# The first weight tile of the output projections: all rounded parts first, then all rests

## The chip, the core and the metric

The kernel runs on one core of a Trainium2 chip. Its engines are TensorE (PE: matmuls, with weight loads shown apart as PEld), VectorE (DVE), ScalarE (ACT), GpSimd (POOL) and SyncE (SP, which issues the loads). Each engine works through its own list of instructions in order and waits on semaphores for the others. The metric is the device time of one execution in microseconds (us); the kernel before takes 3476.52 us, the median of 3 runs (3475.16 to 3477.75).

## The reference, cut to what matters

The reference is two transformer blocks of two layers each, on 512 tokens of width 1024; the second block also carries 256 context tokens. Each of the four layers has a mixer (attention heads in layers 0, 2 and 3, a gated delta rule in layer 1), an output projection, and a feed-forward part:

```
mixed = concat(heads) @ w_out          # 1024 x 1024, in every layer
x = x + gate * mixed
h = rmsnorm(x, g) * (1.0 + scale) + shift
x = x + gate_f * swiglu(h, w_in, w_out)
```

The change touches only `concat(heads) @ w_out`. In layers 2 and 3 two of the eight head chunks are normalised before it (the differential attention's `rmsnorm_2(o, subln_g)`). In layer 2 the projection is done for the 512 tokens and the 256 context tokens, in the others for the 512 tokens.

## The kernel before, in words

Activations lie with their features on the 128 partitions: eight chunks ("heads" in the code, each 128 features) of 512 or 768 token columns. The weights of an output projection come in four tiles of 1024 x 256, each giving two blocks (j = 0 and 1) of 128 output features.

A product of full precision is made from rounded numbers. Each operand is split into a rounded part (HI) and a rest (LO), and three products are added up in one PSUM bank: HI·HI, HI weight · LO activation, LO weight · HI activation. ACT writes the rounded parts (weights `W_HI`, heads `O_HI`), POOL subtracts to get the rest of the weights (`W_LO`), DVE to get the rest of the heads (`O_LO`). One (head, j) pair thus costs three matmuls of 128x512; one weight tile for 512 tokens is 8 x 2 x 3 = 48 of them.

The first tile (m = 0) of a projection is special, since the heads have only just been computed. ACT takes it in four pieces (`PIECES`): it rounds a quarter of the weight tile (line 555), then the two heads that go with it (line 526), four times over; in layers 2 and 3 the normalisation of heads 4 and 5 lies between the first piece and the second (lines 2875 and 2876 on ACT, 2882 on DVE, after sums on PE at line 2866). After the last head ACT loads another function table (line 529) and rounds the second tile (line 378), POOL then takes that tile's rest (line 390). DVE splits the heads in the same order (line 589), POOL the four weight pieces (line 565). PE runs `pe_out`: for each group of `side_by_side` heads it first issues the HI·HI products (line 483), each head behind a wait for `heads_rounded`, and then the two products with rests (lines 493 and 494), each head behind waits for the weight piece's rest (`piece_split`, for the last two heads `tile_split`) and for `heads_split`. In the delta rule's layer (`gdn_out`) the group is all eight heads, in the other three projections (`attn_out`, `out2`, `out3`) it is two.

In `out2` the 256 context columns of tile 0 follow by `pe_three` (lines 434 to 436, matmuls of 128x256). Tiles 1 to 3 use `pe_three` for everything, behind a wait for their own `tile_split`. When tile m is done, DVE adds it into X (line 601) and ACT rounds tile m + 2 into the buffer that has come free; squares of X (line 804 on ACT, sums at line 814 on POOL) feed the next norm, whose last sums are made by PE (line 826).

Of the kernel before, what the change touches and what calls it, by code (L numbers as in the profile page):

```python
# [15 lines left out]
DC = D // P  # L16
# [76 lines left out]
def build_program(nc, w_tiles, d_tiles, xT, ctxT, positions, consts, params, rope_tables, outT):  # L93
# [12 lines left out]
    with ctx:  # L106
# [90 lines left out]
        def sig(name):  # L197

            if name not in scratch:
                scratch[name] = sem(name)  # L200
            return scratch[name]
# [60 lines left out]
        def base(who, name, count):  # L262


            key = (who, name)
            at = BASE.get(key, 0)
            BASE[key] = at + count
            return at
# [159 lines left out]
        def pe_three(pe, o, w, hi, lo, x_hi, x_lo, n, wait=None):  # L428


            for k in range(n):
                if wait:
                    wait(k)
                pe.matmul(PS[:, o:o + w], hi(k), x_hi(k), start=k == 0, stop=False)  # L434
                pe.matmul(PS[:, o:o + w], hi(k), x_lo(k), start=False, stop=False)  # L435
                mm = pe.matmul(PS[:, o:o + w], lo(k), x_hi(k), start=False, stop=k == n - 1)  # L436
            return mm
# [22 lines left out]
        def heads_order(name):  # L460

            return [0, 1, 2, 3, 6, 7, 4, 5] if name in ("out2", "out3") else list(range(DC))

        def pe_out(pe, name, segs):
            e0 = E0[name]
            b_r = base("pe", "heads_rounded", DC)
            b = base("pe", "heads_split", DC)
            b_p = base("pe", "piece_split", PIECES - 1)
            heads = heads_order(name)
            side_by_side = DC if name == "gdn_out" else 2  # L470
            col = lambda k, j: slice(k * 256 + j * P, k * 256 + (j + 1) * P)
            for m in range(OWN[name]):
                hi, lo = W_HI[:, (SPLIT[name] + m) % 2, :], W_LO[:, (SPLIT[name] + m) % 2, :]
                pe.wait_ge(evac_done, e0 + m - 1)
                later = segs
                if m == 0:

                    (c0, w), later = segs[0], segs[1:]
                    for p0 in range(0, DC, side_by_side):
                        for p in range(p0, p0 + side_by_side):  # L480
                            pe.wait_ge(sig("heads_rounded"), b_r + p + 1)
                            for j in range(2):
                                pe.matmul(PS[:, out_column(m, j, c0):out_column(m, j, c0) + w], hi[:, col(heads[p], j)],
                                          O_HI[:, heads[p], c0:c0 + w], start=p == 0, stop=False)
                        for p in range(p0, p0 + side_by_side):
                            if p // 2 < PIECES - 1:
                                pe.wait_ge(sig("piece_split"), b_p + p // 2 + 1)
                            else:
                                pe.wait_ge(sig("tile_split"), SPLIT[name] + 1)
                            pe.wait_ge(sig("heads_split"), b + p + 1)  # L490
                            for j in range(2):
                                to = PS[:, out_column(m, j, c0):out_column(m, j, c0) + w]
                                pe.matmul(to, hi[:, col(heads[p], j)], O_LO[:, heads[p], c0:c0 + w], start=False, stop=False)
                                mm = pe.matmul(to, lo[:, col(heads[p], j)], O_HI[:, heads[p], c0:c0 + w], start=False,
                                               stop=p == DC - 1)
                                if p == DC - 1 and not later:
                                    mm.then_inc(tile_done if j else sig("out_first_done"), 1)
                    if not later:
                        continue
                else:  # L500
                    pe.wait_ge(sig("tile_split"), SPLIT[name] + m + 1)
                for j in range(2):
                    for c0, w in later:
                        mm = pe_three(pe, out_column(m, j, c0), w, lambda k: hi[:, col(k, j)], lambda k: lo[:, col(k, j)],
                                      lambda k: O_HI[:, k, c0:c0 + w], lambda k: O_LO[:, k, c0:c0 + w], DC)
                    mm.then_inc(tile_done if j else sig("out_first_done"), 1)
            pe_norm_sum(pe, OUT_SUM, sum(w for _, w in segs))
# [4 lines left out]
        def out_column(m, j, c0):  # L512
            return (m % 2) * 1536 + (1024 + j * 256 if c0 else j * 512)
# [302 lines left out]
        def pe_norm_sum(pe, o, w):  # L816
            n = base("pe", "norm_summed", 1)
            for last in range(2):
                if last:
                    pe.wait_ge(sig("norm_squared"), (n + 1) * DC)  # L820
                else:
                    pe.wait_ge(sig("norm_added"), (n + 1) * (DC - 2))
                src = NORM_SQ[:, (DC - 1) % 2, :] if last else NORM_SUM[:, :]
                for c in range(0, w, 512):
                    x = min(512, w - c)
                    mm = pe.matmul(PS[:, o + c:o + c + x], ones, src[:, c:c + x], start=not last, stop=bool(last))
            mm.then_inc(sig("norm_summed"), 1)
# [2130 lines left out]
        def _(pe):  # L2958
            ph = Phase()
            for layer in range(4):  # L2960
                segs = SEG1 if layer < 2 or layer == LAST else SEG2
                if layer == 0:
                    pe_ada0(pe)
                    pe_attn_in(pe)
                    ph.end(pe)
                    pe_stick(pe)
                    ph.end(pe)
                    pe_pairs(pe, causal_tasks())
                    ph.end(pe)
                    pe_out(pe, "attn_out", SEG1)  # L2970
                elif layer == 1:
                    pe_gdn_in(pe)
                    ph.end(pe)
                    pe_gdn_prep(pe)
                    ph.end(pe)
                    pe_gdn_inverse(pe)
                    ph.end(pe)
                    pe_scan(pe)
                    ph.end(pe)
                    pe_gdn_out(pe)  # L2980
                    pe_out(pe, "gdn_out", SEG1)
                else:
                    pe_in(pe, layer)
                    ph.end(pe)
                    pe_conv_norm(pe, layer)
                    ph.end(pe)
                    pe_pairs(pe, mixer_tasks(layer))
                    ph.end(pe)
                    pe_sub_norm(pe, layer)
                    pe_out(pe, f"out{layer}", segs)  # L2990
# [341 lines left out]
```

## Time and profile before

| | us |
|---|---|
| median of 3 runs (range) | 3476.52 (3475.16 to 3477.75) |
| the profiled execution | 3475.19 |
| its span in the trace | 3473.5 |
| PE busy | 3235.7 (93% of the span) |
| DVE, ACT, POOL busy | 1675.4, 1166.2, 1312.2 |
| granted TensorE clock over the span | 0.966 |

Of the profiled time 1.7 us lie outside the span. The granted clock is a share of 2.4 GHz: 1.00 is that level, 0.50 is 1.2 GHz, and a value between is a stretch with both. A matmul's row shows its whole passage; back to back they start closer together than they last, so a run of them is read from start to start. PE is the engine that is busy nearly always. The first tiles of the four projections begin at 342.69, 1160.45, 2032.01 and 3042.21 us of the span.

### The profile page before, as it was taken

What the parts mean: (1) busy time and instruction counts of PE and PEld (TensorE: products, weight loads), DVE (VectorE), ACT (ScalarE), POOL (GpSimd) and SP (SyncE); (2) the same over time, 40 slices, a digit from 0 to 9 for tenths busy, and PEclk for the clock granted to TensorE, in tenths of its full rate; (3) what the DMA queues carried; (4) which work ended last, traced back from release to release, by engine and by line L of the source; (5) the groups of instructions that cost most, each with busy time, mean ns of one, the idle gap of its engine ahead of it and who ended that gap; (6) DMA issues with size and microseconds to landing.
All of it is one profiled execution on the core that took longest, in us unless ns stands there. A gap on an engine that the chain in (4) does not pass through costs nothing. (4 is left out here: it accounts for less than half of the span.)

```text
span 3473.5 us, 43878 instructions
## 1 busy us (share of the span) xinstructions
PE 3235.7 (93%) x16780; PEld 2547.3 (73%) x16780; DVE 1675.4 (48%) x2845; ACT 1166.2 (34%) x1526; POOL 1312.2 (38%) x711
## 2 busy tenths in 40 slices
PE   7998999999976899998997998999999997989998
PEld 6864788878866688886883367888899783368887
DVE  5544442427566474654736625734355737431111
ACT  2244322223362322223234433222344325442222
POOL 3313444444461333433314543343400414544443
PEclk9989999999997899999998999999999998999999
DMA  6510243432201134432110022444344210022321
GB/s 261 192 63 25 109 182 139 189 119 85 72 1 49 61 145 151 169 149 75 62 37 1 1 73 87 173 146 182 139 172 161 92 49 1 25 85 82 106 86 66
DMA packets 54643, 352.91 MB, mean 102 GB/s; under 512 B 5856, under 2 KB 6880, under 8 KB 19552
## 3 DMA queue, kind: packets, MB, share of 16 engines
q1 hardware_dynamic: 54208, 348.79, 27.2%
q8 instruction: 100, 1.64, 0.2%
q10 hardware_dynamic: 288, 2.10, 0.2%
q14 instruction: 47, 0.39, 0.0%
HBM read 348.77 MB, written 2.10 MB: 101 GB/s over the span
## 5 line engine op out<-in xcount | busy, mean ns | idle before, releaser
L390 POOL TENSOR_TENSOR W_LO<-ring,W_HI 128x2048 fp32r<-128x2048 f32 (+1 forms) x177 | 729.4, 4121 | 1063.7 <-ACT W_HI L378 1063.7
L446 PE MATMUL PS<-H_HI,W_HI 128*128 128x512 f32 (+1 forms) x1888 | 712.2, 377 | 28.9 <-DVE H_LO L867 22.0
L448 PE MATMUL PS<-H_HI,W_LO 128*128 128x512 f32 (+1 forms) x1888 | 702.7, 372 | 0.0
L447 PE MATMUL PS<-H_LO,W_HI 128*128 128x512 f32 (+1 forms) x1888 | 702.5, 372 | 0.0
L378 ACT ACTIVATE W_HI<-ring 128x2048 fp32r<-128x2048 f32 (+1 forms) x214 | 366.3, 1712 | 471.2 <-PE PS L436 417.8
L446 PEld LDWEIGHTS PS<-H_HI,W_HI 128*128 128x128 f32 x1888 | 359.2, 190 | 93.0 <-issue 31.5
L448 PEld LDWEIGHTS PS<-H_HI,W_LO 128*128 128x128 f32 x1888 | 358.7, 190 | 63.0
L447 PEld LDWEIGHTS PS<-H_LO,W_HI 128*128 128x128 f32 x1888 | 359.1, 190 | 59.4 <-issue 0.2
L909 DVE SCALAR_TENSOR_TENSOR PS<-ring,SC,PS 128x256 f32<-128x256 f32 x768 | 376.2, 490 | 27.0
L434 PE MATMUL PS<-HID_HI,W_HI 128*128 128x512 f32 (+1 forms) x880 | 325.3, 370 | 4.9 <-DVE W_LO L390 4.0
L436 PE MATMUL PS<-HID_HI,W_LO 128*128 128x512 f32 (+1 forms) x880 | 323.8, 368 | 0.0
L435 PE MATMUL PS<-HID_LO,W_HI 128*128 128x512 f32 (+1 forms) x880 | 323.7, 368 | 0.0
L640 ACT ACTIVATE GATED<-PS 128x512 f32<-128x512 f32 (+1 forms) x110 | 61.1, 555 | 724.8 <-PE PS L448 724.8
L655 DVE TENSOR_TENSOR HIDDEN<-GATED,PS 128x512 f32<-128x512 f32 (+1 forms) x110 | 69.8, 634 | 424.6 <-ACT GATED L640 424.6
L784 DVE SCALAR_TENSOR_TENSOR X<-PS,MOD,X 128x512 f32<-128x512 f32 (+1 forms) x80 | 55.7, 696 | 386.0 <-PE PS L436 386.0
L434 PE MATMUL PS<-H_HI,U_HI 128*128 128x512 f32 x520 | 206.0, 396 | 19.5 <-DVE H_LO L867 14.0
L435 PE MATMUL PS<-H_LO,U_HI 128*128 128x512 f32 x520 | 204.7, 394 | 0.0
L436 PE MATMUL PS<-H_HI,U_LO 128*128 128x512 f32 x520 | 204.4, 393 | 0.0
L434 PEld LDWEIGHTS PS<-HID_HI,W_HI 128*128 128x128 f32 x880 | 165.9, 189 | 34.5 <-DVE W_LO L390 5.3
L436 PEld LDWEIGHTS PS<-HID_HI,W_LO 128*128 128x128 f32 x880 | 165.9, 188 | 27.7
L435 PEld LDWEIGHTS PS<-HID_LO,W_HI 128*128 128x128 f32 x880 | 165.9, 189 | 27.2
L2521 POOL TENSOR_TENSOR U_LO<-ring,U_HI 128x1024 fp32r<-128x1024 f32 x40 | 102.7, 2570 | 214.5 <-ACT U_HI L2509 214.5
(393 smaller groups left out, 5387.6 us busy)
## 6 DMA issues: line engine op xcount, KB each, us to landing
ring<-w_tiles SPq DMA_DIRECT2D x271, 1024.0 KB, 4.8
ring<-d_tiles SPq DMA_DIRECT2D x80, 704.0 KB, 4.1
X<-xT SPq DMA_DIRECT2D x1, 2048.0 KB, 12.5
WORK<-rope_tables ACTq DMA_DIRECT2D x2, 1024.0 KB, 4.9
outT<-H SPq DMA_DIRECT2D x8, 256.0 KB, 2.2
X<-ctxT SPq DMA_DIRECT2D x1, 1024.0 KB, 9.1
CN<-consts SPq DMA_DIRECT2D x1, 931.0 KB, 15.3
PR<-params SPq DMA_DIRECT2D x1, 465.5 KB, 3.5
```

The lines of the kernel that those rows point to most:

```text
L378: act.activation(W_HI[:, b, 0:w], ring[:, g % SLOTS, 0:w], ACT.Copy).then_inc(sig("tile_rounded"), 1)
L390: eng.tensor_tensor(W_LO[:, b, 0:w], ring[:, g % SLOTS, 0:w], W_HI[:, b, 0:w].bitcast(F32), ALU.subtract).then_inc(sig("tile_split"), 1)
L434: pe.matmul(PS[:, o:o + w], hi(k), x_hi(k), start=k == 0, stop=False)
L435: pe.matmul(PS[:, o:o + w], hi(k), x_lo(k), start=False, stop=False)
L436: mm = pe.matmul(PS[:, o:o + w], lo(k), x_hi(k), start=False, stop=k == n - 1)
L446: pe.matmul(to, hi[:, cols(k, j)], x_hi(k), start=k == 0, stop=False)
L447: pe.matmul(to, hi[:, cols(k, j)], x_lo(k), start=False, stop=False)
L448: mm = pe.matmul(to, lo[:, cols(k, j)], x_hi(k), start=False, stop=k == n - 1)
L640: act.activation(GATED[:, v, 0:w], PS[:, v * 1024:v * 1024 + w], ACT.Silu).then_inc(sig("gate_silu"), 1)
L655: dve.tensor_tensor(HIDDEN[:, v, 0:w], GATED[:, v, 0:w], PS[:, v * 1024 + 512:v * 1024 + 512 + w], ALU.mult).then_inc(evac_done, 1)
L909: ins = dve.scalar_tensor_tensor(out=out, in0=w, scalar=c[:, k:k + 1], in1=acc, op0=ALU.mult, op1=ALU.add)
L2521: pool.tensor_tensor(U_LO[:, i % 2, :].rearrange("p (k c) -> p k c", k=DC), half_source(layer, t, j), U_HI[:, i % 2, :].rearrange("p (k c) ...
```

## The change

In all four projections the group of heads of tile 0 is now all eight. The number of matmuls, their operands and what they add up to stay as they are; only their order on PE and the places of PE's waits differ, and only in `attn_out`, `out2` and `out3`.

```
             heads = heads_order(name)
-            side_by_side = DC if name == "gdn_out" else 2
+            side_by_side = DC
             col = lambda k, j: slice(k * 256 + j * P, k * 256 + (j + 1) * P)
```

PE's list in `out2`, before, from the sums of the sub-norm (line 2866) to the third head's rounded part; in brackets stands what an instruction waits for:

```order
L2866 MATMUL PS<-BIG,CN 128x256
L483 MATMUL PS<-O_HI,W_HI 128x512 [waits heads_rounded,evac_done]
L483 MATMUL PS<-O_HI,W_HI 128x512
L483 MATMUL PS<-O_HI,W_HI 128x512 [waits heads_rounded]
L483 MATMUL PS<-O_HI,W_HI 128x512
L493 MATMUL PS<-O_LO,W_HI 128x512 [waits heads_split,piece_split]
L494 MATMUL PS<-O_HI,W_LO 128x512
...
L483 MATMUL PS<-O_HI,W_HI 128x512 [waits heads_rounded]
```

Where the dots stand are six more products with rests: eight of them lie between the rounded parts of the second head and of the third. The same place after the change, to the first product with a rest:

```order
L2866 MATMUL PS<-BIG,CN 128x256
L483 MATMUL PS<-O_HI,W_HI 128x512 [waits heads_rounded,evac_done]
L483 MATMUL PS<-O_HI,W_HI 128x512
L483 MATMUL PS<-O_HI,W_HI 128x512 [waits heads_rounded]
L483 MATMUL PS<-O_HI,W_HI 128x512
...
L493 MATMUL PS<-O_LO,W_HI 128x512 [waits heads_split,piece_split]
L494 MATMUL PS<-O_HI,W_LO 128x512
```

Where the dots stand are the twelve rounded products of the third to the eighth head, each head behind its own wait for `heads_rounded`. The number of instructions is the same; the lists of DVE, ACT, POOL and SP are the same row for row.

## Rows read from the trace of the kernel before

**Rows 1.** The page: the span, and the granted clock in 40 slices.

```profile
span 3473.5 us, 43878 instructions
PEclk9989999999997899999998999999999998999999
```

**Rows 2.** Timeline, PE, out2: start, length, engine, line, operands [idle before <-releaser].

```profile
2032.01 1.63 PE L483 MATMUL PS<-O_HI,W_HI 128*128 128x512 f32 x4
...
2035.69 1.47 PE L483 MATMUL PS<-O_HI,W_HI 128*128 128x512 f32 x4 [0.22 <-ACT O_HI L526]
...
2037.53 0.47 PE L493 MATMUL PS<-O_LO,W_HI 128*128 128x512 f32 x1 [0.37 <-DVE O_LO L589]
...
2039.50 0.47 PE L493 MATMUL PS<-O_LO,W_HI 128*128 128x512 f32 x1 [0.82 <-DVE O_LO L589]
...
2046.13 0.28 PE L434 MATMUL PS<-O_HI,W_HI 128*128 128x256 f32 x1
```

**Rows 3.** Timeline, ACT, DVE and POOL, out2.

```profile
2034.81 1.56 ACT L526 ACTIVATE O_HI<-H 128x768 fp32r<-128x768 f32 x2
...
2035.67 8.25 DVE L589 TENSOR_TENSOR O_LO<-H,O_HI 128x768 fp32r<-128x768 f32 x6 [0.24 <-ACT O_HI L526]
...
2038.79 1.56 ACT L526 ACTIVATE O_HI<-H 128x768 fp32r<-128x768 f32 x2
2038.96 1.54 POOL L565 TENSOR_TENSOR W_LO<-ring,W_HI 128x512 fp32r<-128x512 f32 x1 [0.43 <-ACT W_HI L555]
...
2043.67 4.73 POOL L390 TENSOR_TENSOR W_LO<-ring,W_HI 128x2048 fp32r<-128x2048 f32 x1 [3.17 <-ACT W_HI L378]
```

**Rows 4.** Timeline, PE, gdn_out: first product with a rest, and tile 1's first.

```profile
1165.05 0.39 PE L493 MATMUL PS<-O_LO,W_HI 128*128 128x512 f32 x1
...
1172.30 0.39 PE L434 MATMUL PS<-O_HI,W_HI 128*128 128x512 f32 x1
```

**Rows 5.** Windows, tile 1 of out2: us, busy of PE, PEld, DVE, ACT, POOL, PEclk, DMA, GB/s.

```profile
2051.80:2068.00 16.20, 16.20 (x95) 14.28 (x94) 2.19 (x4) 3.40 (x3) 6.43 (x2) 1.00 0.24 83
```

**Rows 6.** Timeline, PE, the norm behind out2.

```profile
2106.07 2.93 PE L826 MATMUL PS<-NORM_SUM,CN 128*128 128x512 f32 x4 [3.99 <-POOL NORM_SUM L814]
```

**Rows 7.** Timeline, PE, ACT and POOL, attn_out.

```profile
342.69 1.66 PE L483 MATMUL PS<-O_HI,W_HI 128*128 128x512 f32 x4 [3.55 <-ACT O_HI L526]
...
346.62 1.14 ACT L526 ACTIVATE O_HI<-H 128x512 fp32r<-128x512 f32 x2
...
351.07 4.90 POOL L390 TENSOR_TENSOR W_LO<-ring,W_HI 128x2048 fp32r<-128x2048 f32 x1 [2.53 <-ACT W_HI L378]
...
355.44 0.39 PE L494 MATMUL PS<-O_HI,W_LO 128*128 128x512 f32 x1
...
356.12 0.47 PE L434 MATMUL PS<-O_HI,W_HI 128*128 128x512 f32 x1 [0.29 <-POOL W_LO L390]
```

**Rows 8.** Timeline, ACT, POOL and PE, out3.

```profile
3048.15 1.13 ACT L526 ACTIVATE O_HI<-H 128x512 fp32r<-128x512 f32 x2
...
3052.60 4.59 POOL L390 TENSOR_TENSOR W_LO<-ring,W_HI 128x2048 fp32r<-128x2048 f32 x1 [2.68 <-ACT W_HI L378]
...
3055.14 0.39 PE L494 MATMUL PS<-O_HI,W_LO 128*128 128x512 f32 x1
...
3057.33 0.47 PE L434 MATMUL PS<-O_HI,W_HI 128*128 128x512 f32 x1 [1.80 <-POOL W_LO L390]
```

**Rows 9.** Timeline, PE: two pauses of nearly one length.

```profile
1228.26 1.05 PE L925 MATMUL PS<-SM,ACC 128*128 128x1 f32 x8 [2.75 <-DVE ACC L909]
...
2132.41 1.05 PE L925 MATMUL PS<-SM,ACC 128*128 128x1 f32 x8 [2.59 <-DVE ACC L909]
```

**Rows 10.** Windows: behind these two pauses, and one of out2.

```profile
1230.60:1234.00 3.40, 3.40 (x9) 2.63 (x8) 3.15 (x8) 0.66 (x1) 2.66 (x1) 0.50 0.96 359
...
2131.70:2140.00 8.30, 7.59 (x37) 6.44 (x38) 6.99 (x15) 2.44 (x2) 4.50 (x1) 1.00 0.64 247
...
2039.00:2040.00 1.00, 0.50 (x2) 0.48 (x3) 1.00 (x2) 1.00 (x2) 1.00 (x1) 1.00 0.00 0
```

## The prediction, made before the changed kernel ran

> **What bounds the kernel now.** I read the page first. PE is busy 93% of the span and its clock is near the upper level almost everywhere [rows 1], so what counts is PE's own list: a microsecond that PE loses is lost, unless it would have waited anyway. The change touches three places of that list, so I then read the timeline of each, PE beside ACT, DVE and POOL. Three questions are put to each place: when does tile 0 end now, what paces it, and what does tile 1 wait for?
>
> The clearest place is out2, in layer 2 [rows 2, 3]. PE has the first two heads' rounded products out of the way by 2033.6 (2032.01 + 1.63). Then ACT is held up by the norm of heads 4 and 5, and the third head is rounded only at about 2035.6: L526 starts at 2034.81 and takes 1.56 for two heads. PE fills that hole with the eight rest products of the first two heads, and its wait before 2035.69 is 0.22 us. It has two more waits, 0.37 and 0.82 us, both for the rests of heads from DVE. The whole of tile 0 for 512 columns takes from 2032.01 to 2046.13, 14.1 us.
>
> **What 48 matmuls cost.** The delta rule's projection already runs the new order, but there all heads are rounded by the time PE comes. From its first rest product to tile 1's first product are 7.25 us for 32 matmuls, without a gap [rows 4], or 0.227 us each at the upper clock. So 48 need 10.9 us, and tile 0 of out2 now loses 3.2 us to waits and to the lower clock at its start.
>
> **The change, part by part.** No instruction is added or removed, and the four other engines keep their lists. PE's rest products move behind all rounded products. So the new order has a simple lower end: tile 0 can't end before (the last head is rounded) + 2 rounded products + 32 rest products, since the rest products, 7.25 us of work, now all stand behind the wait for the eighth head. A matmul starts 0.10 us behind the rounding that it waits for (2035.59 to 2035.69, rows 2 and 3).
>
> Out2: the last head is rounded at 2038.79 + 1.56 = 2040.35 [rows 3]. Then 0.10 + 2 x 0.227 + 7.25 = 7.8 us, so the rest products end at 2048.15, where before the next work began at 2046.13 [rows 2]. That is +2.0 us. The rests are not late in that sum: POOL has the last weight piece at 2038.96 + 1.54 = 2040.5, and DVE the last head at 2035.67 + 8.25 = 2043.92, while PE asks for it 28 products behind the start of the rest products, at about 2047. Nothing covers the 2.0 us. The 256 context columns follow at once in either kernel, and in tile 1 PE is busy for the whole 16.20 of 16.20 us [rows 5]: it doesn't wait there for POOL, whose W_LO is ready at 2043.67 + 4.73 = 2048.4 [rows 3]. Behind out2 comes the norm, a strict chain from PE over DVE, ACT and POOL back to PE [rows 6], which moves as a whole. What the later end of tile 0 holds up on the other engines is the addition into X and the rounding of tile 2, both 2.0 us later; tile 2 is wanted a whole tile later, some 16 us on.
>
> Attn_out: the last head is rounded at 346.62 + 1.14 = 347.76, and 7.8 us more give 355.56. Before, the last product of tile 0 started at 355.44 and its successor could start at 355.67, but tile 1 begins at 356.12, because POOL has its rest only at 351.07 + 4.90 = 355.97 [rows 7]. Both orders end ahead of that, so the change is worth 0, and with the same reason nothing could be gained there.
>
> Out3: the last head at 3048.15 + 1.13 = 3049.28, and 7.8 us more give 3057.08. Before, tile 0's products were through at 3055.14 + 0.23 = 3055.37, so tile 0 gets 1.7 us longer. But tile 1 waits for POOL until 3052.60 + 4.59 = 3057.19 and starts at 3057.33 [rows 8]: PE's wait of 1.80 us covers it, with 0.25 us to spare. Here 0. If that cover were gone, it would cost 1.7. Tile 2 is rounded 1.7 us later and is again wanted a whole tile (10.9 us) later, when ACT and POOL need under 7 for it.
>
> The three sums together give +2.0 us: 3475.19 + 2.0 = 3477.2 for the profiled execution. That one stood 1.33 below the median of the three runs, so as a median I say 3476.52 + 2.0 = 3478.5 us, or +0.06%. The runs of before spread over 2.6 us; 0.2%, 7 us, is about what a measurement of this kernel can tell from no change.
>
> **What the trace does not show** is PE's clock under the new order. In out2 PE will pause from 2033.6 to 2035.7 and then get two matmuls (0.45 us of work) at a time, about every 0.8 us with longer gaps between pairs of heads, until 2040.4. Two rows bound it. A pause of 2.59 us left the clock at 1.00 for what followed, a pause of 2.75 us of the same instruction brought it to 0.50 from 1230.60 to 1234.00 [rows 9, 10]. So a fall costs up to 3.4 us at half the pace, 1.7 us, and it may cost nothing if it lies where PE waits for heads. For the sum I take the clock held, as the new pause (2.1 us) is the shorter and as the clock stayed at 1.00 in out2 with PE half idle from 2039 to 2040 [rows 10]. Both ends, 0 and 1.7 us for each of out2 and out3, stay in the range.
>
> **The rivals.** First, the clock falls in out2 or out3. It costs up to 1.7 us in each, less in out3, where 0.25 us is covered: the kernel would come out at +3 to +5.5 us. For it speaks the row at 1230.60, against it the row at 2131.70. The Trainium skill speaks for it too (TensorE: Matmul & The Clock Gate, section Loop structure matters more than you think): a loop in which matmuls wait each time for their input lets the engine go cold, and they run at the lower clock. The row at 2039.00 does not agree so far, with 0.50 busy and 1.00 granted. I give this 24%.
>
> Second, the slower side: the low clock comes in all three projections, in attn_out by lasting on from its start into the rest products. Three times 1.7 with the 2.0 of out2 is 7.1 us, 3484 us: slower by just over 0.2%. It decides only if each fall lies wholly in dense rest products. Nothing but the price of one fall speaks for it. Against it: attn_out's first four products take 1.66 us, and ACT rounds the next two heads in 1.14 [rows 7], so PE has hardly a pause there. 4%.
>
> Third, PE gains. Of the 3.2 us that tile 0 of out2 loses now, 1.4 are waits for heads and rests (0.22, 0.37, 0.82). If their cause were the order on PE, the new order would win them back: -1.4 us, at the most -3.2 with the start-up. Against it stands the lower end worked out above, in which 7.8 us follow the last head. It would need ACT to get through its heads earlier, and ACT waits for nothing that PE does in this order. 7%.
>
> Fourth, no effect: the 2.0 us are given back, say by POOL and DVE not getting into each other's way at the new times. ACT, DVE and POOL have the same lists and no new waits, so I see no mechanism; 10% for within 1 us of before.
>
> **How the numbers follow.** The forecast of +2.0 us has 55%, with its own range of +1 to +3. The clock rival has 24%, no effect 10%, the gain 7%, the slower side 4%. The range is to hold 8 in 10: it reaches down to 3475.0, which takes in no effect and half of the gain together with the spread of the runs, and up to 3483.0, which is the top of the clock rival (3482.0) with 1 us for the runs' own spread. Slower by over 0.2% means over 3483.5: the second rival, 4%. Faster by over 0.2% means under 3469.6, more than any reading of these waits would give; 1% for what I have not seen. The rest, 95%, is within 0.2%.
>
> **What would show it.** In the changed kernel's timeline of out2, the first rest product should start at about 2040.9 with no wait at any later one, the first 128x256 product near 2048.15, 2.0 later than before against the start of L483, and tile 1 should follow it without a wait. In attn_out and out3 tile 1 should still wait for POOL and start 13.4 and 15.1 us behind the first rounded product; in out3 the wait shrinks from 1.80 to about 0.25. The granted clock in the six microseconds behind out2's second rounded head should read 1.00. I am wrong if tile 1 of out3 starts later than POOL's rest, if PE's rest products wait for DVE, or if the clock reads 0.50 there.

## The result, and the profile after

| us | before | after |
|---|---|---|
| median (range), 9 runs each | 3475.44 (3471.01 to 3477.75) | 3483.74 (3480.94 to 3490.34) |
| the profiled execution | 3475.19 | 3480.94 |
| its span | 3473.5 | 3479.2 |

The ratio is 1.0026 (95% interval 1.0015 to 1.0036); like the ratios below it is an estimate from the runs and not the quotient of the two medians, which is 1.0024. The change costs 8.3 us by the medians, and each of the nine runs is above all nine of before. The forecast was +2.0 us with a range up to 3483.0. The profiled execution is the quickest of the nine, so its trace holds 5.7 of the 8.3 us.

The page of the kernel after, span and granted clock, to be read against [rows 1]: the digits of the clock hardly differ and don't tell where the loss is.

```profile
span 3479.2 us, 43878 instructions
PEclk9999999999997899999998999999999998999999
```

The timeline of PE in out2 (start, length, engine, line, operands, idle before) is to be read against [rows 2]:

```profile
2031.10 1.67 PE L483 MATMUL PS<-O_HI,W_HI 128*128 128x512 f32 x4
...
2034.79 5.45 PE L483 MATMUL PS<-O_HI,W_HI 128*128 128x512 f32 x12 [2.02 <-ACT O_HI L526]
...
2040.08 0.40 PE L493 MATMUL PS<-O_LO,W_HI 128*128 128x512 f32 x1
...
2047.35 0.28 PE L434 MATMUL PS<-O_HI,W_HI 128*128 128x256 f32 x1
```

Nothing waits behind the last head. Tile 0 takes 2047.35 - 2031.10 = 16.25 us against 14.12 before, 2.13 us more; 2.0 was forecast. (In three of the other profiles with this order, all_three, only_out2 and out2_busy, it takes 16.03 to 16.07 us, 1.9 more.) The rest products take 7.27 us (2040.08 to 2047.35), as in the delta rule's layer.

The same in out3, PE and POOL, against [rows 8]:

```profile
3047.95 2.05 PE L483 MATMUL PS<-O_HI,W_HI 128*128 128x512 f32 x4
...
3058.33 4.61 POOL L390 TENSOR_TENSOR W_LO<-ring,W_HI 128x2048 fp32r<-128x2048 f32 x1 [2.69 <-ACT W_HI L378]
...
3062.71 0.39 PE L494 MATMUL PS<-O_HI,W_LO 128*128 128x512 f32 x1
3063.09 0.47 PE L434 MATMUL PS<-O_HI,W_HI 128*128 128x512 f32 x1
```

Tile 0 takes 15.14 us against 15.12. PE has just finished (3062.71 + 0.23) when POOL has (3058.33 + 4.61 = 3062.94), so the cover of 1.80 us is used up. In attn_out tile 1 starts 13.43 us behind the first product in both kernels, still behind POOL:

```profile
341.95 5.85 PE L483 MATMUL PS<-O_HI,W_HI 128*128 128x512 f32 x16 [3.55 <-ACT O_HI L526]
...
355.38 0.47 PE L434 MATMUL PS<-O_HI,W_HI 128*128 128x512 f32 x1 [0.31 <-POOL W_LO L390]
```

So all three places did what was forecast, and together they explain 2.1 us. To find the rest, take the same instruction in both traces and look at how far it has moved. Where that number jumps, time was lost.

| instruction | before | after | moved by |
|---|---|---|---|
| out2, first product (L483) | 2032.01 | 2031.10 | -0.91 |
| out2, end of tile 0 (L434, 128x256) | 2046.13 | 2047.35 | +1.22 |
| X of out2's last tile (DVE L601) | 2102.12 | 2103.34 | +1.22 |
| first tile of the up projection, layer 2 (L925) | 2132.41 | 2132.62 | +0.21 |
| last sum of the norm before layer 3 (L826) | 2705.50 | 2707.44 | +1.94 |
| sums of layer 3's convolution (L2643) | 2849.88 | 2853.19 | +3.31 |
| out3, first product (L483) | 3042.21 | 3047.95 | +5.74 |
| end of the span | 3473.5 | 3479.2 | +5.7 |

From out2's start to the end that is 6.6 us: 2.1 in tile 0, 1.0 given back between the end of out2 and the up projection, where the norm lies, and then 1.7, 1.4 and 2.4 us lost in three stretches that the change doesn't touch. (The -0.91 at the start is how far two executions drift apart anyway: across all profiles below, the work ahead of out2 ends between 2023 and 2030.) Here are the windows at those places after; columns are us, busy time of PE, PEld, DVE, ACT, POOL with the instructions, granted clock, DMA share, GB/s:

```profile
2134.30:2137.70 3.40, 3.40 (x9) 2.67 (x8) 3.22 (x7) 1.32 (x1) 2.00 (x1) 0.50 0.80 284
...
2707.70:2714.50 6.80, 6.09 (x15) 4.28 (x15) 4.41 (x8) 3.32 (x7) 3.65 (x2) 0.50 0.01 2
...
2861.30:2868.10 6.80, 6.80 (x38) 3.46 (x38) 4.56 (x7) 1.83 (x2) 0.00 (x0) 0.50 0.00 0
```

And the same stretches of before:

```profile
2133.30:2136.70 3.40, 3.40 (x17) 2.79 (x17) 2.79 (x6) 2.12 (x2) 1.20 (x1) 1.00 0.57 190
...
2707.20:2714.00 6.80, 6.80 (x30) 5.63 (x31) 6.12 (x12) 3.32 (x7) 2.24 (x1) 1.00 0.01 2
...
2858.80:2862.20 3.40, 3.40 (x12) 1.67 (x9) 2.81 (x5) 1.83 (x2) 0.00 (x0) 0.50 0.00 0
2862.20:2865.60 3.40, 3.40 (x41) 1.61 (x40) 0.96 (x3) 2.10 (x3) 0.00 (x0) 1.00 0.00 0
```

9 matmuls stand against 17 in 3.4 us, 15 against 30 in 6.8: PE runs at 1.2 GHz where it ran at 2.4 before, 90, 680 and 830 us behind tile 0 of out2. At 2134 nothing covers the loss. At 2708 it is partly covered: PE falls 2.5 us further behind before by 2710.93, and 1.1 of them are gone again at the product that starts at 2719.26 in before, where PE waits 0.91 us for POOL's rest of the weights and after doesn't wait. Of the 2.4 us of the third row 1.6 are lost in the stretch from 2861.3; the other 0.8 come up to 2912, where both kernels have the same time at the lower clock (24 us), but over other instructions.

Inside out2 the clock fell too, in this profile, behind the third head; in the window 2035.30 to 2038.70 it reads 0.50, and 1.00 in the one behind:

```profile
2035.30:2038.70 3.40, 3.37 (x7) 1.62 (x6) 3.40 (x3) 3.40 (x7) 2.58 (x3) 0.50 0.00 0
...
2040.00:2047.00 7.00, 7.00 (x33) 5.77 (x32) 3.01 (x4) 2.67 (x2) 4.24 (x1) 1.00 0.46 150
```

That fall cost nothing: PE has only two products per rounded head to do there, and the first rest product began within 0.1 us of where it was forecast.

### The profile page after: what moved, and what is told of

Read it like the earlier page. It is cut to its first block and busy times, and to the rows that moved or that the text cites. A ratio compares the mean times of both kernels' runs of the same rounds, so it can differ in the third digit from the quotient of the medians.

```text
span 3479.2 us, 43878 instructions
## 1 busy us (share of the span) xinstructions
PE 3239.1 (93%) x16780; PEld 2550.2 (73%) x16780; DVE 1674.9 (48%) x2845; ACT 1166.3 (34%) x1526; POOL 1312.3 (38%) x711
## 5 line engine op out<-in xcount | busy, mean ns | idle before, releaser
L434 PE MATMUL PS<-HID_HI,W_HI 128*128 128x512 f32 (+1 forms) x880 | 325.3, 370 | 4.9 <-DVE W_LO L390 4.0
L434 PE MATMUL PS<-H_HI,U_HI 128*128 128x512 f32 x520 | 207.0, 398 | 18.3 <-DVE H_LO L867 13.9
L434 PEld LDWEIGHTS PS<-HID_HI,W_HI 128*128 128x128 f32 x880 | 165.9, 189 | 34.7 <-DVE W_LO L390 5.3
```

## The experiments

Two theories were to be told apart. **Place:** the new order itself costs more than its tiles show, in one of the projections or by what the projections do together. **Shift:** the order costs 2.1 us and no more; but whatever makes the program behind out2 late by that much moves its later pauses, and some of them then lose the clock. A rival to both was chance, as the profile after is one execution.

The matmuls added in these kernels write a bank that is free there, and nothing reads their results; where lines were added, the line numbers behind them are higher (L928 or L936 is L925 of before).

**One projection at a time.** Each of the three kernels changes one projection; the fourth is the change once more, on the same chip.

```
-            side_by_side = DC if name == "gdn_out" else 2
+            side_by_side = DC if name in ("gdn_out", "out2") else 2        # only_out2
+            side_by_side = DC if name in ("gdn_out", "attn_out") else 2    # only_attn_out
+            side_by_side = DC if name in ("gdn_out", "out3") else 2        # only_out3
+            side_by_side = DC                                              # all_three
```

> The changed kernel again, to have it beside its parts. Local theory (each projection pays what its timeline shows: 0 in attn_out, +2.0 in out2, 0 in out3): +2 us against the kernel before, about 1.0006. Clock theory (on top of that the new pauses bring TensorE's clock to 1.2 GHz in out2 and out3 in most executions, though not in the one profiled): +5 to +8 us, and a profiled execution may show 0.50 in one of the two. Later-stage theory (the shift sets off a loss behind the projection, the same in every execution): +6 to +8 us with the clock at 1.00 in the three tiles.

> Only attn_out takes the new order. Local theory: 0, since tile 1 waits for POOL in either order. Clock theory: 0 to +0.8 us, as PE has hardly a pause there. Later-stage theory: up to +2 us, for the start of later stages moves.

> Only out2 takes the new order. Local theory: +2.0 us, out2's tile 0 takes 16.2 us instead of 14.1 and nothing else moves. Clock theory: +3 to +4 us, the longest of the new pauses (2.0 us) is here. Later-stage theory: +4 or more with tile 0 at 16.2 us.

> Only out3 takes the new order. Local theory: 0, tile 1 begins 15.1 us behind the first rounded product in either order, since POOL has its rest only then. Clock theory: +1 to +2 us, for the cover is only 0.25 us. Later-stage theory: 0 to +2 us.

Against 3474.65 us for before on this chip:

| kernel | median, us | ratio (95%) | span of the profiled one |
|---|---|---|---|
| all_three | 3485.10 | 1.0031 (1.0019 to 1.0043) | 3483.5 |
| only_out2 | 3483.24 | 1.0027 (1.0016 to 1.0038) | 3483.7 |
| only_attn_out | 3475.28 | 1.0004 (0.9995 to 1.0013) | 3471.3 |
| only_out3 | 3475.23 | 1.0002 (0.9993 to 1.0011) | 3473.4 |

The cost is out2's, all of it, and it is there again on another chip. Only_out2 falls at the same three places as the change:

```profile
2135.40:2142.30 6.90, 6.39 (x19) 5.43 (x20) 5.70 (x12) 2.43 (x2) 3.31 (x1) 0.51 0.44 169
...
2712.30:2719.20 6.90, 6.18 (x15) 4.38 (x15) 4.54 (x9) 3.32 (x7) 3.62 (x2) 0.51 0.01 2
...
2866.00:2873.00 7.00, 7.00 (x42) 3.35 (x40) 4.37 (x7) 1.90 (x3) 0.00 (x0) 0.52 0.00 0
```

All_three does so as well (at 2135.2, 2712.0 and 2865.6); only_attn_out and only_out3 have neither of the first two. So it isn't the chance of one profile. At 2134 the low stretch is longer in these two (6.8 us, after has 3.4) and costs 2.9 to 3.0 us in place of 1.7; all_three's profile, whose time of 3485.27 is close to its median, is thus the better account of the usual execution of the change. This leaves open whether out2's order or its lateness does it.

**The old order, only late.** These three keep the order of before and put 5, 9 or 15 matmuls behind tile 0's products of out2. The fourth has the new order in out2 and 6 matmuls more.

```
+                    if name == "out2":
+                        for _ in range(9):      # 5, 9, 15; 6 in out2_plus6
+                            pe.matmul(PS[:, 1536:2048], hi[:, col(0, 0)], O_HI[:, 0, 0:T], start=True, stop=True)
                     if not later:
                         continue
```

> The same with 5 more matmuls, 1.1 us. Shift theory: anything between +1 and +8, the point between no delay (0) and 9 matmuls. Order theory: +1.1 us.

> The old order everywhere; behind the 512-column part of out2's tile 0 PE gets 9 more matmuls of 128x512 into a free bank, back to back (9 x 0.227 = 2.0 us, the same delay as the change brings there). Shift theory (what costs more than the 2.0 us is not the order, but that all that follows runs 2.0 us later against the moments at which TensorE's clock is set): +7 to +10 us, and the falls of the clock at 2135, 2712 and 2866 us are there again. Order theory (the rest is lost by something that the new order does to out2): +2.0 us and no such falls.

> The same with 15 more matmuls, 3.4 us. Shift theory: the cost does not grow with the delay; a delay of another size meets the clock at other moments, and as 6.8 us is what two stretches at the lower level last here, I expect that half of it puts the later stages back where they were: +3.4 us, less than with 9, and the clock as in the kernel before. Order theory, and any theory of a later stage that only wants time: +3.4 us at least, and more than with 9.

> Only out2 has the new order (+8.6 us when it ran alone), and on top of it 6 more matmuls, 1.4 us, so that everything behind is 3.4 to 3.5 us later than before. Shift theory: +3.5 us, so 5 us faster than the new order without the additional work. Order theory: +10 us, 8.6 + 1.4.

In the timeline of PE the added matmuls take 9 x 0.227 = 2.0 us and 15 x 0.227 = 3.4 us. Their group rows, from delay9 and delay15, show that they run at the upper clock:

```profile
2042.73 2.20 PE L500 MATMUL PS<-O_HI,W_HI 128*128 128x512 f32 x9
```

```profile
2045.97 3.56 PE L500 MATMUL PS<-O_HI,W_HI 128*128 128x512 f32 x15
```

Against 3475.33 us for before on this chip:

| kernel | out2 later by, us | median, us | ratio (95%) | span |
|---|---|---|---|---|
| delay5 | 1.1 | 3477.99 | 1.0008 (0.9999 to 1.0017) | 3480.4 |
| delay9 | 2.0 | 3484.23 | 1.0023 (1.0014 to 1.0032) | 3479.1 |
| delay15 | 3.4 | 3478.74 | 1.0008 (0.9999 to 1.0017) | 3475.7 |
| out2_plus6 | 3.5 (2.1 + 1.4) | 3479.22 | 1.0008 (0.9999 to 1.0018) | 3478.4 |

(One of out2_plus6's eleven runs took 13822 us, which no trace explains; the median hardly feels it.)

This decides between the two theories. Delay9 has the old order and costs as much as the change, +8.9 us by the medians. Out2_plus6 has the new order and more work than the change, and costs 3.9 us, less than half. With 3.4 us of delay the cost by the medians is about the delay and nothing more. Delay9 falls where the change falls (and again at 2861.3):

```profile
2131.00:2137.60 6.60, 6.45 (x19) 5.49 (x20) 5.39 (x11) 2.43 (x2) 3.37 (x1) 0.50 0.50 180
...
2707.70:2714.50 6.80, 6.02 (x15) 4.34 (x14) 4.58 (x8) 3.32 (x7) 3.56 (x2) 0.50 0.01 2
```

Delay15 keeps the clock at both places:

```profile
2135.80:2142.60 6.80, 6.80 (x31) 5.63 (x31) 6.04 (x13) 2.02 (x2) 4.62 (x1) 1.00 0.80 308
...
2709.00:2716.00 7.00, 6.40 (x28) 5.33 (x29) 5.71 (x11) 3.49 (x8) 2.86 (x2) 1.00 0.01 2
```

So does out2_plus6:

```profile
2138.00:2145.00 7.00, 7.00 (x35) 5.89 (x35) 5.78 (x12) 2.44 (x2) 4.40 (x1) 1.00 0.72 286
...
2711.00:2718.00 7.00, 6.00 (x27) 4.75 (x26) 4.99 (x9) 3.40 (x8) 3.57 (x2) 1.00 0.01 2
```

Delay5 is between: five of its runs lie from 3473.50 to 3476.05, five from 3479.62 to 3483.17, one between. The profiled one is of the upper group and has the falls (2135.5, 2709.0, 2862.6). A lower one has no profile, so that the lower group is the one without falls is likely, not shown. The clock over the whole span, which is on record for every run, points the same way: 0.966 is the mean of the lower five, 0.964 of the upper five.

Whether the clock falls at 2134 is not told by the length of the pause. The row of L925 stands for the pause ahead of it, in brackets. In the kernel after:

```profile
2132.62 1.05 PE L925 MATMUL PS<-SM,ACC 128*128 128x1 f32 x8 [3.10 <-DVE ACC L909]
```

In only_out2:

```profile
2135.91 1.86 PE L925 MATMUL PS<-SM,ACC 128*128 128x1 f32 x8 [2.49 <-DVE ACC L909]
```

In delay9:

```profile
2131.15 1.86 PE L928 MATMUL PS<-SM,ACC 128*128 128x1 f32 x8 [2.39 <-DVE ACC L912]
```

In delay15:

```profile
2134.81 1.05 PE L928 MATMUL PS<-SM,ACC 128*128 128x1 f32 x8 [2.62 <-DVE ACC L912]
```

And in out2_plus6:

```profile
2137.51 1.05 PE L928 MATMUL PS<-SM,ACC 128*128 128x1 f32 x8 [2.66 <-DVE ACC L912]
```

Pauses of 2.39, 2.49 and 3.10 us lost the clock, and pauses of 2.59 [rows 9], 2.62 and 2.66 us kept it. Nor is it the time since the start of the span: 2131.15 lost, 2132.41 kept, 2132.62 lost, 2134.81 kept. The rows also show that the fall has no fixed place against the pause: the eight small matmuls take 1.86 us in only_out2 and delay9, where the clock was low before the pause was over, and 1.05 in after, where the window from 2130.90 to 2134.30 still reads 1.00 and the fall comes 1.7 us behind the pause.

The second place shows it more plainly, as its pause has one length. In the norm ahead of layer 3 PE waits 2.03 us at the same instruction in all these profiles. In before, with the clock kept:

```profile
2705.50 0.70 PE L826 MATMUL PS<-NORM_SQ,CN 128*128 128x256 f32 x2 [2.03 <-ACT NORM_SQ L804]
```

And in after, with the clock lost:

```profile
2707.44 0.97 PE L826 MATMUL PS<-NORM_SQ,CN 128*128 128x256 f32 x2 [2.03 <-ACT NORM_SQ L804]
```

In delay15 and out2_plus6 the 2.03 us kept the clock, in all_three, only_out2, delay9 and delay5 they lost it.

Does the lateness behind out2 sort them? To measure it, take the same instruction ahead of out2 in each profile (DVE L1462, at 2022.27 in before; L1465 where lines were added) and count from it, in us more than in before:

| profile | to L925 (L928) | clock at 2134 | to the end of the span |
|---|---|---|---|
| only_out3 | -1.43 | kept | -1.4 |
| only_attn_out | +0.03 | kept | 0.0 |
| delay15 | +2.00 | kept | +1.9 |
| out2_plus6 | +2.03 | kept | +1.8 |
| delay5 | -0.51 | lost | +5.0 |
| after | +1.11 | lost | +6.6 |
| all_three | +1.27 | lost | +8.0 |
| only_out2 | +1.65 | lost | +8.4 |
| delay9 | +1.55 | lost | +8.4 |

The last column falls in two groups, -1.4 to +1.9 without the fall and +5.0 to +8.4 with it. Within 1.1 to 1.7 us of lateness the clock was lost, at 0 and at 2.0 it was kept; but the profiled delay5 came there 0.5 us early and lost it, and only_out3, in which nothing of layer 2 is changed, 1.4 us early and kept it. So executions differ here by more than a microsecond by themselves, and the delay that was put in is not a sure guide for a single one.

**Work in the pauses.** If the low stretches are the loss, then matmuls in the two pauses ahead of them must bring the time back. Out2_busy has the new order in out2 and 9 matmuls in the pause before L925 and 8 in the one before L826; before_busy has them in the old order.

```
+                        for v in range(2):              # first pair of up200, out of the loop
+                            product(v, 2 * v, 0)
+                            if v == 0:
+                                for _ in range(9):
+                                    pe.matmul(PS[:, 1024:1536], H_HI[:, 0, 0:P], H_HI[:, 0, :], start=True, stop=True)
...
                 if last:
+                    for _ in range(busy):               # 8 for down211
+                        pe.matmul(PS[:, 1024:1536], HID_HI[:, 0, 0:P], HID_HI[:, 0, :], start=True, stop=True)
                     pe.wait_ge(sig("norm_squared"), (n + 1) * DC)
```

> Only out2 has the new order, and PE gets work into a free bank in the two pauses behind which the clock fell in every profile with a late out2: 9 matmuls in the pause of 2.5 us in layer 2's first feed-forward tile, 8 in the pause of 2.0 us in the last norm ahead of layer 3. Shift theory (the price beyond 2.0 us is paid by these falls and those that follow in layer 3): both falls are gone from the profile, that gives back 3 to 3.5 us at once, and the kernel is at +2 to +5.5 us instead of +8.6. Rival (the falls at 2135 and 2712 us only go along with the loss): +8.6, or a little more by what the added work costs.

> The kernel before with the same work in the two pauses, where its profile shows no fall. Both theories: within 1 us of the kernel before. If it is faster by 1.5 us or more, the kernel before pays for such falls in part of its executions.

Against 3476.02 us for before on this chip: out2_busy's median is 3480.21 us, ratio 1.0009 (1.0000 to 1.0018), span 3478.9; before_busy's is 3474.70, ratio 0.9997 (0.9988 to 1.0006), span 3472.6. In out2_busy's timeline only 0.32 us are left of the first pause, of 2.5 to 3.1:

```profile
2135.01 2.20 PE L628 MATMUL PS<-H_HI 128*128 128x512 f32 x9
2137.53 1.05 PE L936 MATMUL PS<-SM,ACC 128*128 128x1 f32 x8 [0.32 <-DVE ACC L920]
```

And both stretches read 1.00, under the order that lost them in only_out2:

```profile
2136.00:2145.00 9.00, 8.69 (x43) 7.03 (x42) 7.65 (x16) 2.45 (x2) 4.30 (x2) 1.00 0.57 217
...
2712.00:2720.00 8.00, 7.70 (x34) 6.40 (x35) 7.01 (x14) 4.22 (x9) 2.56 (x2) 1.00 0.01 2
```

With the clock kept there, the cost of out2's order falls from 1.0027 to 1.0009, 8.6 to 4.2 us by the medians (on two chips); the intervals overlap only from 1.0016 to 1.0018. The third place then reads as in before, with one stretch of 3.4 us at 0.50 from 2864.2, though nothing was added there. In the profiled execution the time from DVE L1462 ahead of out2 to the end is 1.8 us longer than in before, about tile 0's own cost. In before the same work makes no difference clear of noise. But against before_busy, which has the same added work, out2_busy is 5.5 us slower by the medians and not 4.2, so the part of the cost that the pauses account for is 3.1 to 4.4 of the 8.6 us. Its runs spread from 3470.63 to 3485.35; where the rest goes in the slower ones no profile shows.

**Can tile 0 of out2 be had cheaper?** Its first products run at the lower clock, as PE waits for the sums of the sub-norm. These two kernels keep the old order and give PE 13 matmuls behind the attention's pairs, in layer 2 alone or in layers 2 and 3.

```
+                    if layer in (2,):                   # (2, 3) in warm_both
+                        pe_keep_busy(pe, mixer_tasks(layer), 13)
...
+            for _ in range(count):
+                pe.matmul(PS[:, a:a + T], MINUS[:, :], MAX_ROWS[:, 0, :], start=True, stop=True)
```

> The kernel before with 13 matmuls into a free bank at the end of the attention phase of layers 2 and 3, where PE sits idle for 5.0 and 4.1 us ahead of the sub-norm's sums. If the clock holds, the sums take about half of their 5.5 and 3.7 us, and tile 0 starts at the upper clock: -2 to -2.8 us in out2 and -1 to -1.8 in out3 by their own timelines. Shift theory: what is left at the end is not that sum, as all behind moves against the clock: anything from -7 to +1 us. Rival (local sums add up): -3 to -4.6 us.

> The same in layer 2 alone. Local sum: -2 to -2.8 us. Shift theory: an advance meets the clock at other moments as a delay does, 0 to -4 us.

Warm_both is 3477.66, ratio 1.0002 (0.9993 to 1.0011), warm_out2 3482.16, ratio 1.0008 (0.9999 to 1.0017). At its own place the edit does what it should. In the timeline of warm_out2 the sub-norm's first four sums last 1.53 us:

```profile
2025.82 3.26 PE L1388 MATMUL PS<-MAX_ROWS,MINUS 128*128 128x512 f32 x13
...
2030.92 1.53 PE L2877 MATMUL PS<-BIG,CN 128*128 128x512 f32 x4 [1.85 <-DVE BIG L2870]
...
2047.89 0.28 PE L434 MATMUL PS<-O_HI,W_HI 128*128 128x256 f32 x1
```

From the last pair's matmul to the context columns it takes 22.4 us against 24.4 before, 2.0 gained. But the clock of the profiled execution then falls at 2135.5, 2712.4 and 2862.6, like that of the change, and besides at 2674.8, where that of the change stays up, and it is slower than before. Two of these windows:

```profile
2135.50:2138.90 3.40, 3.40 (x10) 2.62 (x9) 3.19 (x7) 0.83 (x1) 2.49 (x1) 0.50 0.94 335
...
2712.40:2715.80 3.40, 3.40 (x10) 2.62 (x9) 3.40 (x6) 1.25 (x3) 1.17 (x1) 0.50 0.00 0
```

A shift of 2 us the other way thus meets the same three places and a fourth, and its eleven runs fall into two groups as delay5's do (3474.37 to 3476.81 and 3482.16 to 3484.83). No kernel of this study is faster than before by more than can be measured.

## Why the prediction was wrong

**Right, and confirmed.** The lower end of tile 0 (last head, two products, 32 rest products) makes it 2.13 us longer, 2.0 forecast. The first rest product stands 8.98 us behind the first L483, 8.9 forecast, and no rest product waits for DVE or for POOL's pieces. Attn_out is covered (13.43 us in both) and out3 is covered (15.14 and 15.12); only_attn_out and only_out3 show no cost in the time either.

**The clock in out2.** The text said it should read 1.00 and that 0.50 would prove it wrong. It read 0.50 from 2035.3 to 2038.7 in one of the five profiles with this order in out2 (the change's own; not in all_three, only_out2, out2_plus6 or out2_busy). The price in that place was nought, the lower of the two bounds given: PE waits for heads there.

**The step that failed** is the sentence that behind out2 comes the norm, a strict chain "which moves as a whole", and with it the sum's silence on everything further on: all that lies behind tile 0 of out2 stood in it at nothing. That was taken from the dependencies: a strict chain from PE over DVE, ACT and POOL back to PE, the same lists, the same waits. The chains held; but the clock at which PE runs them did not stay with them. The missing term is 1.7 + 1.4 + 2.4 us at 2134, 2708 and 2861, less 1.0 given back in the norm, where after has 10.2 us at the lower clock between 2104 and 2122 and before 13.6. With it the sum is 2.1 + 4.5 = 6.6 us in the profiled execution, the quickest of the nine. The median's 8.3 us are near the 8.0 of all_three's profile, where the norm gives nothing back and the fall at 2135 costs 2.9.

**Why it was missed.** The evidence was in [rows 9, 10]: of two pauses before L925, 2.75 us lost the clock and 2.59 us kept it. They were read as a price for the new pause in out2, in that tile only. The right question was put to neither: which pauses of this length lie behind the change, on PE's own path, and at what clock does before come out of each? There are three, ahead of 2132, 2705 and 2850, the first two kept in before. (The third is the least sure: its stretch at 0.50 starts 9 us behind that pause in before and 8 us behind it in after, so that it belongs to this pause isn't shown.) At the 1.7 us of one fall each they give a range of +2 to +7.1 us, and more where a fall lasts longer, and the rival "slower by over 0.2%" would have had much more than 4%. That rival forecast 3484, close to the result, but put the falls into the three projections, which is not where they are.

**Shown, inferred, open.** Shown: the loss beyond tile 0 is not the order's, since the old order with 2.0 us of delay costs as much (delay9) and the new order with 1.4 us more work costs less than half (out2_plus6). Shown too: matmuls in the two pauses take away the low stretches and, by the medians, 3.1 to 4.4 of the 8.6 us. Inferred: the moments at which the clock can change don't move with the program, so that a shift changes which part of a pause they meet. It agrees with the 2.03 us pause that loses the clock in some profiles and keeps it in others, with the fall that comes before the end of the pause in one profile and behind it in another, and with the two groups of times. When the clock did change the windows show; a moment at which it could have and didn't leaves no row. Open: what put the profiled delay5 among the losers, why the cost at 3.4 us of delay is so much smaller than at 2, and how much of the spread of single runs comes from this.

## What to carry to other kernels

Where PE is the bound, a few microseconds added or saved are not the end of the sum: list the pauses on PE that lie behind the change, with the granted clock behind each, and give a price for each that could tip. To read such a difference, follow the same instruction through both traces until its offset jumps, and compare the windows there. Before an order is blamed or praised for a few microseconds, run the old order with the same delay, and with another.

## What the runs showed of the hardware

A local loss of 2 us cost 8 to 10 (8.3 in the change, 10.4 in all_three, 8.6 in only_out2, 8.9 in delay9), one of 3.4 us cost 3.4 to 3.9 (delay15, out2_plus6), one of 1.1 us 2.7 with runs in two groups (delay5), and a local gain of 2.0 us brought none (warm_out2, ratio 1.0008): the total doesn't simply grow with the delay. (All by the medians; in the profiles of delay15 and out2_plus6 it is 1.9 and 1.8 us.) Pauses of 2.39, 2.49 and 3.10 us were followed by a clock of 0.50, pauses of 2.59, 2.62 and 2.66 us of the same instruction by 1.00, and a pause of 2.03 us at one and the same instruction by either, so the length of a pause within these bounds doesn't tell whether the clock falls. A low stretch costs what PE has to do in it: 3.4 us at 0.50 cost nothing in out2, where PE waited for heads, and 1.7 us at 2134, where it had dense work. Keeping PE busy through the two pauses with 17 matmuls cost nothing that can be measured (0.9997, 0.9988 to 1.0006).
